# Two of three groups of modulation columns moved from matmuls to vector multiply-adds

## What is computed

```python
def trunk_layer(x, cond, rows, row_len, s0_f, s0_b, p):
    mod = (jax.nn.silu(cond) @ w_mod + b_mod)[:, None, :]
    sh1, sc1, g1, sh2, sc2, g2 = jnp.split(mod, 6, axis=-1)
    h = rmsnorm(x, norm1_w) * (1 + sc1) + sh1
    ... = jnp.split(h @ w_in, points, axis=-1)
    y_conv = gate_b * conv3_rows(gate_c * u_in, conv_w, conv_b, rows, row_len)
    y_gla, s_f, s_b = gla_mixer(q, k, v, g_out, ...)
    merged = (jax.nn.sigmoid(gate_br_conv) * (y_conv @ w_br_conv)
              + jax.nn.sigmoid(gate_br_gla) * (y_gla @ w_br_gla))
    x = x + g1 * (merged @ w_out)
    h2 = rmsnorm(x, norm2_w) * (1 + sc2) + sh2
    x = x + g2 * moe(h2, ...)
```

## Time and profile before

| | us |
|---|---|
| median of three runs | 1013.08 |
| lowest, highest | 1011.85, 1014.72 |
| the profiled execution, its own time | 1015.14 |
| its span, first to last instruction | 1013.4 |
| PE busy in the span | 930.0 (92%) |
| DVE busy in the span | 367.5 (36%) |
| mean granted PE clock | 0.975 of full |

### The profile page before, as it was taken

One profiled execution on the slowest core, in us unless ns is written; L12 is line 12 of the kernel. 1 busy time (PEld: TensorE's weight loads), 2 busy tenths in 40 slices (PEclk: granted clock), 3 DMA queues, 4 the chain that ended last, 5 costly groups with the idle time before them and its releaser, 6 DMA issues.

```text
span 1013.4 us, 13026 instructions
## 1 busy us (share of the span) xinstructions
PE 930.0 (92%) x4917; PEld 479.7 (47%) x4917; DVE 367.5 (36%) x721; ACT 186.6 (18%) x283; POOL 104.0 (10%) x207
## 2 busy tenths in 40 slices
PE   4999999999999999989999999988988897988795
PEld 0455557586555578644444444433433343433232
DVE  3229513157000324533344333332332232332266
ACT  2140500112001002203212222221221121221111
POOL 2000000000000000010222221111211121211100
PEclk9999999999999999999999999998999999998898
DMA  9846663613363269799999999999999999999994
GB/s 374 289 170 232 231 220 125 209 41 113 95 265 110 83 253 420 306 390 374 365 373 420 421 419 419 421 420 420 419 420 421 422 421 420 420 419 421 422 420 196
DMA packets 82384, 324.25 MB, mean 320 GB/s; under 512 B 10350, under 2 KB 39194, under 8 KB 52368
## 3 DMA queue, kind: packets, MB, share of 16 engines
q1 hardware_dynamic: 66864, 289.43, 71.5%
q0 software_dynamic: 10080, 24.44, 6.2%
q10 hardware_dynamic: 5376, 9.52, 2.7%
HBM read 301.52 MB, written 34.11 MB: 331 GB/s over the span
## 4 chain that ended last, share of the span: by engine, by line
PE 84%; DMA 5%; issue 5%; DVE 4%; ACT 2%; SPq 1%; DVEq 0%
PE bank L527 26%; PE bank L1708 21%; PE bank L556 13%; PE bank L1883 4%; PE bank L1870 4%; DMA arena<-expert_rows 3%; PE bank L514 2%; PE bank L1910 2%; PE bank L1693 2%; PE bank L1785 2%; DMA arena<-in_w_mod_dram 2%; PE bank L545 1%; ACT arena L538 1%; DVE arena L541 1%; PE bank L487 1%
## 5 line engine op out<-in xcount | busy, mean ns | idle before, releaser
L527 PE MATMUL bank<-arena 128*32 128x512 f32 (+2 forms) x1536 | 268.0, 616 | 33.6 <-issue 32.6
L1708 PE MATMUL bank<-arena 128*128 128x384 f32 x640 | 209.9, 488 | 0.0
L527 PEld LDWEIGHTS bank<-arena 128*32 128x32 f32 (+2 forms) x1536 | 94.1, 127 | 204.7 <-issue 203.9
L1708 PEld LDWEIGHTS bank<-arena 128*128 128x128 f32 x640 | 120.8, 190 | 91.4 <-issue 10.0
L556 PE MATMUL bank<-arena 128*32 128x512 f32 (+2 forms) x768 | 133.2, 600 | 6.5 <-issue 5.9
L556 PEld LDWEIGHTS bank<-arena 128*32 128x32 f32 (+2 forms) x768 | 45.2, 124 | 71.4 <-issue 71.4
L569 ACT ACTIVATE arena<-arena 128x1024 f32<-128x1024 f32 x36 | 41.3, 1148 | 166.2 <-DVE arena L565 163.6
L561 DVE SCALAR_TENSOR_TENSOR arena<-bank,arena 128x512 f32<-128x512 f32 x36 | 27.0, 751 | 109.6 <-PE bank L556 109.5
L541 DVE TENSOR_TENSOR arena<-arena,bank 128x256 f32<-128x256 f32 x36 | 21.8, 605 | 113.9 <-ACT arena L538 113.9
L501 POOL DMA_INDIRECT arena<-h_rows,arena x36 | 38.2, 1061 | 240.3 <-issue 124.1
L538 ACT ACTIVATE arena<-bank 128x256 f32<-128x256 f32 x36 | 22.2, 618 | 204.6 <-PE bank L527 204.6
(11 more groups left out here) (250 smaller groups left out, 743.3 us busy)
## 6 DMA issues: line engine op xcount, KB each, us to landing
arena<-in_w_gate_e_dram SPq DMA_DIRECT2D x64, 1024.0 KB, 26.6
arena<-in_w_up_e_dram SPq DMA_DIRECT2D x64, 1024.0 KB, 29.3
arena<-in_w_down_e_dram SPq DMA_DIRECT2D x64, 1024.0 KB, 29.3
arena<-in_w_mod_dram SPq DMA_DIRECT2D x24, 1024.0 KB, 8.2
arena<-in_w_in_dram SPq DMA_DIRECT2D x22, 1024.0 KB, 6.2
expert_rows<-arena SPq DMA_DIRECT2D x6, 2048.0 KB, 23.6
arena<-expert_rows SPq DMA_DIRECT2D x12, 1024.0 KB, 24.9
arena<-mod_rows_out ACTq DMA_DIRECT2D x4, 1024.0 KB, 8.2
```

The costliest lines, as they stand in the source:

```text
L527: ins = pe.matmul(bank[off:off + width, :], x_T[:, k, off:off + width], w[:, :, k, :], start=(k == 0), stop=(k == KT - 1))
L1708: ins = pe.matmul(ps[:, 0:TOK], w[:, k, P * (n % 2):P * (n % 2) + P], hT[:, k, :], start=(k == 0), stop=(k == KT - 1))
```

## The change

The matmuls of groups 1 and 2 go away. Instead DVE multiplies each of their units by the condition's value of its partition and adds it to an accumulator `mod_acc` of 128 x 2 x 2048 (`add_modulation`: for each of the two conditions one instruction of 2048 columns, a `tensor_scalar` for k = 0 and a `scalar_tensor_tensor` for the seven others, so 16 instructions a group). When the eight units are in, PE sums over the partitions (`sum_modulation`): eight matmuls of 512 columns a group, with a stationary operand of two columns that holds a column of ones and one of zeros. `mod_acc` lies on the memory of `states` and `xn`, and of the rows that POOL clears, so `mod_bias(1)` now stands before the heads, and POOL's clearing waits for `("mod", 2)`.

Group 1 is added on DVE among and behind the factors, and summed on PE between the kt transposes and the first scores. Group 2 is added after `gla_ready`, and summed on PE between gbg 5 and gbg 6. The modulation units are loaded later: after k0, k1, q0, q1, v1, go0, go1, gbc0 (group 1) and gbc0 to gbg2 (group 2). SP frees their buffers when DVE has added them (`mod_unit_added`). ACT makes seven of the eight gates of gbg before it stores the rows, and spreads them behind the last gate.

```diff
@@ def mods_after(unit):
-    places = [("u", 0), ("u", 1), ("gc", 0), ("gc", 1), ("gc", 1), ("gb", 0), ("gb", 1), ("gb", 1),
+    places = [("k", 0), ("k", 1), ("q", 0), ("q", 1), ("v", 1), ("go", 0), ("go", 1), ("gbc", 0),
...
@@ def plan_jobs():
     jobs += [("kt", d, h) for d in range(2) for h in range(NH)]
+    jobs += [("mod", 1)]
...
-    jobs += [("gbg", n) for n in range(KT)]
+    jobs += [("gbg", n) for n in range(6)] + [("mod", 2)] + [("gbg", n) for n in range(6, KT)]
@@ banks
-    bank_of = {("xT", 4): 6, ("xT", 5): 7, ("mod", 1): 6, ("mod", 2): 7}
+    bank_of = {("xT", 4): 6, ("xT", 5): 7}
...
+    for j, after in zip(apart, (("kt", 1, 1), ("gbg", 1))):
+        bank_of[j] = bank_of[after]
@@ new
+        def add_modulation(eng, g, k, link):
+            u = ("mod", g, k)
+            unit_arrived(eng, u)
+            for s in range(2):
+                if k == 0:
+                    ins = eng.tensor_scalar(mod_acc[:, s, :], unit_view(u), scond[:, s, 0:1], None, ALU.mult)
+                else:
+                    ins = eng.scalar_tensor_tensor(out=mod_acc[:, s, :], in0=unit_view(u), scalar=scond[:, s, k:k + 1],
+                                                   in1=mod_acc[:, s, :], op0=ALU.mult, op1=ALU.add)
+            link(ins)
+            eng.sem_inc(S["mod_unit_added"], 1)
+            if k == KT - 1:
+                eng.sem_inc(S["mods_added"], 1)
@@ pool_experts
             pool.wait_ge(S["gla_ready"], 1)
+            full(pool, ("mod", 2))
             link(pool.memset(no_rows, 0.0))
@@ vector_part_a
             dve.sem_inc(S["conv_done"], 1)
-            mod_bias(1)
             for d in range(2):
                 for n, f in enumerate((tail_f, key_f, qry_f, cum)):
+                    if d == 0 and n % 2 == 0:
+                        for k in (n, n + 1):
+                            add_modulation(dve, 1, k, link)
                     dve.wait_ge(S["exp_ready"], 4 * d + n + 1)
...
-            mod_bias(2)
+            for k in range(4, KT):
+                add_modulation(dve, 1, k, link)
+            mod_bias(1)
             dve.wait_ge(S["state_in"], 16)
...
             dve.sem_inc(S["gla_ready"], 1)
+            for k in range(KT):
+                add_modulation(dve, 2, k, link)
+            mod_bias(2)
@@ block.sync
-                    if old[0] == "mod" and old[2] < KT - 1:
-                        sp.wait_ge(S["mod_unit_used"], (KT - 1) * old[1] + old[2] + 1)
+                    if old[0] == "mod" and old[1]:
+                        sp.wait_ge(S["mod_unit_added"], KT * (old[1] - 1) + old[2] + 1)
+                    elif old[0] == "mod" and old[2] < KT - 1:
+                        sp.wait_ge(S["mod_unit_used"], old[2] + 1)
@@ block.scalar
             gate("gbc", g_conv)
+            gate("gbg", g_gla, range(KT - 1))
             act.wait_ge(S["mod_ready"], 2)
...
-            gate("gbg", g_gla, spread_mods)
+            gate("gbg", g_gla, [KT - 1])
+            spread_mods()
@@ block.tensor
+            def sum_modulation(g):
+                job = ("mod", g)
+                ps = start(job)
+                pe.wait_ge(S["mods_added"], g)
+                for s in range(2):
+                    for q in range(4):
+                        ins = pe.matmul(ps[32 * q:32 * q + 2, :], chosen_row[:, s, :], mod_acc[:, s, 512 * q:512 * q + 512],
+                                        start=(s == 0), stop=(s == 1), skip_group_check=True)
+                finish(ins, job)
...
-                    if n % 2:
-                        for m in mods_after(u):
-                            modulation(m)
...
-            for i in range(2):
-                for m in mods_after(("v", i)):
-                    modulation(m)
             project("go", CT)
...
+            sum_modulation(1)
             pe.wait_ge(S["fac_ready"], 8)
...
-            project("gbg", KT)
+            project("gbg", 6)
+            sum_modulation(2)
+            project("gbg", KT, 6)
```

More of the change, by code:

```diff
@@ L95, in mods_after @@
 def mods_after(unit):
-    places = [("u", 0), ("u", 1), ("gc", 0), ("gc", 1), ("gc", 1), ("gb", 0), ("gb", 1), ("gb", 1),
-              ("k", 0), ("k", 1), ("k", 1), ("q", 0), ("q", 1), ("q", 1), ("v", 1), ("v", 1)]
+    places = [("k", 0), ("k", 1), ("q", 0), ("q", 1), ("v", 1), ("go", 0), ("go", 1), ("gbc", 0),
+              ("gbc", 0), ("gbc", 1), ("gbc", 2), ("gbc", 3), ("gbg", 0), ("gbg", 1), ("gbg", 2), ("gbg", 2)]
     return [("mod", 1 + n // KT, n % KT) for n, place in enumerate(places) if place == unit]
@@ L109, in plan_units @@
     for name in ("gbc", "gbg"):
-        units += [(name, i) for i in range(4)]
+        for i in range(4):
+            units += [(name, i)]
+            units += mods_after((name, i))
     units += [("wbc", 0), ("wbg", 0), ("wbc", 1), ("wbg", 1)]
@@ L158, in program @@
     jobs = plan_jobs()
-    bank_of = {("xT", 4): 6, ("xT", 5): 7, ("mod", 1): 6, ("mod", 2): 7}
[L160 to L164, removed]
+    bank_of = {("xT", 4): 6, ("xT", 5): 7}
+    turn_of = {("xT", 4): 0, ("xT", 5): 0}
+    taken = [0] * 6 + [1] * 2
+    apart = [("mod", 1), ("mod", 2)]
+    in_turn = [j for j in jobs if j not in apart]
+    early, late = in_turn.index(("go", CT - 1)) + 1, in_turn.index(("sgu", 0))
+    late_bank = [7, 0, 1] + [2 + n % 5 for n in range(len(in_turn) - late - 3 - 2 * NT)] + [3, 4, 5, 6, 3, 4]
+    for n, j in enumerate(in_turn):
         bank_of[j] = n % 6 if n < early else (n - early) % 8 if n < late else late_bank[n - late]
+    for j, after in zip(apart, (("kt", 1, 1), ("gbg", 1))):
+        bank_of[j] = bank_of[after]
+    for j in jobs:
         turn_of[j] = taken[bank_of[j]]
@@ L265, in program @@
         states = at(a_x, 2 * NH, 4, P)
+        mod_acc = at(a_x, 2, 2 * D)
         g2_rows = at(take(2048), 2, D)
@@ L302, in program @@
         rows_in = at(take(P), P)
-        eye32 = at(take(32), 32)
+        chosen_row = at(take(4), 2, 2)
+        take(28)
         modT = at(take(96), 4, 4, 2)
@@ L1459, in _ @@
             link(pool.iota(part_i, pattern=[[0, 1]], base=0, channel_multiplier=1))
+            link(pool.memset(chosen_row, 0.0))
+            for n in range(2):
+                link(pool.memset(chosen_row[:, n, n:n + 1], 1.0))
             link(pool.memset(ones_b, 1.0))
@@ L1580, in _, with gate @@
             act.dma_start(new_state[0, 0].rearrange("w h k v -> k (w h) v"), new_st).then_inc(S["out_done"], 16)
-            def gate(name, dst, also=None):
-                for n in range(KT):
-                    if n == 1 and also:
-                        also()
+            def gate(name, dst, tiles=range(KT)):
+                for n in tiles:
                     full(act, (name, n))
@@ L1691, in modulation @@
                 for q in range(4):
-                    m, cond = (2, scond[:, :, k]) if u[1] else (32, cond_cols[:, k, :])
-                    ins = pe.matmul(ps[32 * q:32 * q + m, :], cond, unit_view(u)[:, 512 * q:512 * q + 512],
+                    ins = pe.matmul(ps[32 * q:32 * q + 32, :], cond_cols[:, k, :], unit_view(u)[:, 512 * q:512 * q + 512],
                                     start=(k == 0), stop=(k == KT - 1), skip_group_check=True)
```

8 lines of the change are left out of this document (5 added, 3 removed).

## The result

| | before | after |
|---|---|---|
| median of the runs | 1013.9 us (1011.85 to 1014.88, 4 runs) | 1001.82 us (1000.61 to 1003.5, 4 runs) |
| ratio, 95% interval | | 0.9889 [0.9869, 0.9908] |
| profiled execution, its own time | 1015.14 us | 1002.71 us |
| its span, mean granted clock | 1013.4 us, 0.975 | 1001.0 us, 0.976 |

What follows compares the result with a forecast made beforehand. PE was taken to bound the projections without a gap. Removed matmuls, sums and stall, -15.0 + 3.7 + 1.8 = -9.5 us, gave 1003.6 us from the median of 1013.1; range 1000.2 to 1006.8.

Steps and rivals of the forecast that it cites:

- What bounds the kernel: From 42 to 204 us PE works without a gap; each us of PE work removed there is a us of time.
- What goes: Modulation matmuls between the projections: six units alone at 0.97 us, five pairs at 1.83 us, 15.0 us off the chain.
- The sums, 2 x 1.83: PE's two sums over the partitions, one per group, both on its chain: 3.7 us added, at least 1.9.
- DVE's price and slack: Group 1 on DVE: 2.33 us per 2048-column addition, the last done 2.7 us before PE comes to the sum.
- Twice-priced additions: Rival: additions at 4.9 us instead of 2.33 make PE wait 9.2 us and the gain is gone; chance 0.03.
- a late last addition: Rival: PE waits at group 1's sum for the last unit, costing 1 to 3 us, 1004.6 to 1006.6; chance 0.14.
- The first head, +3.6: First head out at T + 11.55 instead of T + 7.92, T being the end of kt: 1.83 sum, the rest stall.
- a stall of 1.8: First head: PE newly waits 1.8 us because the bias addition delays DVE's masked scores; bounds 0 and 2.3.
- The clock: End of the heads: granted clock was 0.80 from 236 to 244 us, 1.6 us lost, which a shifted rhythm might avoid.
- rival "absorbed": The heads' slack absorbs the stall and the clock doesn't fall at their end: 1000.2 to 1001.8 us; chance 0.12.
- the forecast's own bounds: Whole kernel: 1002.3 to 1004.8 us around the forecast of 1003.6, given a chance of 0.62.
- Given back later: Rival: the gain is lost in an experts' stage paced by DMA, leaving 1011 to 1013 us; chance 0.05.

Runs made afterwards that it cites:

- e_unit7: The changed kernel with two more additions of 2048 columns on DVE behind the last unit of group 1, into unused memory; 1003.87 us.
- e_sum_late: e_act_bias with group 1's sum moved behind the first head's scores, into a bank whose next user comes later; 1001.65 us, ratio to before 0.9887.
- e_act_bias: The changed kernel, but ACT copies group 1's sum out of its bank and DVE adds the bias after group 2; 1001.0 us, ratio to before 0.9887.

## Why the prediction was right, and which term was off

- **What bounds the kernel.** Right. PE's stretch of projections gave one us for one.
- **What goes, "6 x 0.97 + 5 x 1.83 = 15.0".** This is the term that was mis-sized: it measured 17.0. The sum counted the rows of the modulation matmuls and took the projections' rows between them as unchanged. The projection right behind an interruption was 0.20 us longer, ten times. It could be read from the rows: the earlier trace rows has 82.56 us for 16 undisturbed columns, 5.16 each, so four are 20.64, and the earlier trace rows had the four of `go` with 20.84 right behind an interruption. 20.65 came after.
- **The sums, 2 x 1.83.** Right: 1.94 (0.11 more on the chain) and 1.83. The second one is itself an interruption, so the pair behind it has the 0.20 us too and the gates came to +2.0 (72.24 + 1.83 + 10.52 = 84.59) instead of +1.8.
- **DVE's price and slack.** Additions were put at 2.33 us and took 2.35; 2.7 us of slack for the last one were worked out, and 3.5 were there, of which the hand-over takes 0.3. The Trainium skill's formula for a `tensor_tensor` (VectorE: DVE Perf Modes, "The TRN2 errata") gives 2.29 us, 0.06 less than this `scalar_tensor_tensor` with a scalar per partition took. Twice-priced additions and a late last addition did not occur; `e_unit7` shows that the second is 3.2 us away.
- **The first head, +3.6.** It measured +3.7. The path was right (bias addition, masked scores, state updates), and `e_sum_late` took back 1.85 us where a stall of 1.8 was worked out. What it left out is the bank: with DVE's delay gone, `e_act_bias` was still 1.0 us from the 9.75 that a sum without a stall would give, and the chain there ran over the bank.
- **The clock.** That it doesn't fall at the end of the heads was part of the rival "absorbed", and in the profile compared it did not fall: -1.5 us. The stall was not absorbed, though, and the fall comes and goes between executions of one kernel, so this was no success of that rival.
- **The number.** The median, 1001.82 us, lies 0.5 us below the forecast's own bounds (1002.3 to 1004.8) and at the edge of the rival "absorbed" (to 1001.8). By the total alone that rival would look as good; the traces decide against it. The two large differences, -2.0 of interruptions and -1.5 of clock, point the same way, and of the second it is luck that the profile compared did not have it.
- **Given back later.** No: 0.3 us on the first profile. The stretch from the output projection's start to the end took 648.9 and 649.1 us in the two profiles of before and 649.2, 648.6 and 647.5 in those of the change.

Against the forecast for the profiled execution, 1005.6 us, the differences are -2.0 (interruptions), -1.5 (clock), +0.1 (head), +0.2 (gates) and +0.3 (later): -2.9 us, and it took 1002.7. Without the clock's 1.5 us, which comes and goes, the change is worth 17.0 - 3.7 - 2.0 = 11.3 us, less what varies in the rest of the program.

## What to carry to other kernels

When work is taken out from between the pieces of a bound engine, compare the length of a piece behind an interruption with that of an undisturbed one; the interrupting rows are not the whole price. Work put on an engine with room is free only up to each hand-over, so work out the slack there and not from the busy share; what is on the path is the tail of the hand-over, here a sum, an addition of two partitions' rows and the bank that it holds. Put such a tail behind the next work that someone waits for, and into a bank whose next user is far away.

## What the runs showed of the hardware that I had not expected

- A projection right behind matmuls with a two-column stationary operand takes 0.20 us more than an undisturbed one (10.52 us a pair against 10.32), whether these have 512 columns or 32. Behind matmuls over 32 rows (32x384) it is the same (5.36 us a column against 5.16).
- A wait cost more than itself where the clock fell behind it, in one execution each: 3.43 us of wait came with a granted clock of 0.84 and 0.73 and 2.1 us more in the first head; 15.29 us came with 0.51 and a sum of 3.59 us instead of 1.83.
- Operations on two partitions were as dear as on 128 by their columns. A DVE addition of 2x512 out of a bank took 0.70 us (2.79 for four) and one of 128x384 took 0.56; an ACT copy of 2x512 took 0.59 (2.38 for four) and one of 128x384 0.49.
- The stretch from the output projection's start to the end varied from 646.2 us (`e_act_bias`) to 650.4 (`e_sum_late`) in profiles of kernels that do not differ in it. Its cause stays open; it is larger than the gain of either of these two versions over the change.
